# HGRN2 in a decoder trunk: stacked exponents, cross scores in place of a state, weights rounded on GpSimd, and a new order of calls

## What is computed

```python
q, fz, i, g = jnp.split(x @ w_in, 4, axis=-1)
q = silu(q); f = lower_bound + (1 - lower_bound) * sigmoid(fz)
log_f = jnp.log(f); k = 1 - f
# in each of 8 heads of width 128, b = cumsum(log_f) over tokens:
#   out[t] = sum over s <= t of (sum_k q[t,k] k[s,k] exp(b[t,k] - b[s,k])) v[s]
o = rms_norm(o, g_norm) * silu(g)
return o @ w_o
```

## Time and profile before

| | |
|---|---|
| median of 3 runs | 995.34 us (995.27 to 995.46) |
| the profiled execution's own time | 994.82 us |
| its span, first to last instruction | 993.3 us |
| PE busy | 982.4 us, 99% of the span |
| DVE, ACT, POOL busy | 711.2, 501.1, 38.4 us |
| phase C, roughly | 645 to 798 us of the span |
| TensorE clock granted | 0.999 of full speed |

### The profile page before, as it was taken

One profiled execution on the slowest core, in us unless ns is written; L12 is line 12 of the kernel. 1 busy time (PEld: TensorE's weight loads), 2 busy tenths in 40 slices (PEclk: granted clock), 3 DMA queues, 4 the chain that ended last, 5 costly groups with the idle time before them and its releaser, 6 DMA issues.

```text
span 993.3 us, 13958 instructions
## 1 busy us (share of the span) xinstructions
PE 982.4 (99%) x5116; PEld 829.9 (84%) x5116; DVE 711.2 (72%) x960; ACT 501.1 (50%) x571; POOL 38.4 (4%) x63
## 2 busy tenths in 40 slices
PE   9999999999999999999999999999999999999996
PEld 7888888888888888888888888888888888888885
DVE  5686667785879666668786666788877877565665
ACT  6663544346547544532444343358978535444430
POOL 0100000000210000000000000000001100000000
PEclk9999999999999999999999999999999999999999
DMA  8687655552756656563666464734233657656521
GB/s 296 221 285 243 210 168 193 170 194 103 251 202 235 220 175 205 172 233 122 215 214 210 164 211 168 236 111 145 85 128 125 215 174 239 214 167 210 165 101 42
DMA packets 129255, 184.72 MB, mean 186 GB/s; under 512 B 5952, under 2 KB 104784, under 8 KB 129088
## 3 DMA queue, kind: packets, MB, share of 16 engines
q1 hardware_dynamic: 126032, 173.56, 52.2%
q0 software_dynamic: 2624, 10.11, 2.9%
q10 hardware_dynamic: 560, 0.52, 0.2%
HBM read 183.13 MB, written 1.05 MB: 185 GB/s over the span
## 4 chain that ended last, share of the span: by engine, by line
PE 93%; DVE 2%; ACT 2%; DMA 1%; issue 0%; POOL 0%; DVEq 0%; SPq 0%; ACTq 0%
PE psum L1527 24%; PE psum L1501 17%; PE psum L1503 17%; PE psum L1502 17%; PE psum L1531 12%; PE psum L1975 1%; DMA raw<-in_ffn_w_in 1%; ACT w_hi L429 1%; PE psum L1496 1%; PE psum L1960 1%; PE psum L1644 1%; DVE w_lo L853 0%; PE psum L1940 0%; PE psum L1711 0%; DVE stats L893 0%
## 5 line engine op out<-in xcount | busy, mean ns | idle before, releaser
L853 DVE TENSOR_TENSOR w_lo<-raw,w_hi 128x2048 fp32r<-128x2048 f32 x161 | 367.4, 2287 | 40.7 <-ACT w_hi L429 40.1
L1527 PE MATMUL psum<-xT,w_hi 128*128 128x512 f32 x1024 | 358.5, 396 | 0.0
L429 ACT CAST w_hi<-raw 128x2048 fp32r<-128x2048 f32 x161 | 303.9, 1909 | 26.7 <-DMA raw<-in_ffn_w_in 15.6
L1531 PE MATMUL psum<-xT,w_lo 128*128 128x256 f32 x1024 | 275.7, 280 | 0.0
L1527 PEld LDWEIGHTS psum<-xT,w_hi 128*128 128x128 f32 x1024 | 190.4, 188 | 41.3
L1531 PEld LDWEIGHTS psum<-xT,w_lo 128*128 128x128 f32 x1024 | 192.9, 188 | 5.4
L944 DVE TENSOR_REDUCE ffn_tok<-psum 128x256 f32<-128x512 f32 x128 | 82.4, 686 | 152.3 <-PE psum L1527 152.3
L1501 PE MATMUL psum<-w_hi,xT 128*128 128x512 f32 x447 | 178.8, 400 | 0.8 <-DVE xT L874 0.7
L1503 PE MATMUL psum<-w_hi,xT 128*128 128x512 f32 x447 | 174.7, 391 | 0.0
L1502 PE MATMUL psum<-w_lo,xT 128*128 128x512 f32 x447 | 174.4, 390 | 0.0
L463 ACT ACTIVATE ffn_tok<-ffn_tok 128x256 f32<-128x256 f32 x64 | 26.8, 418 | 233.6 <-DVE ffn_tok L944 233.6
(11 more groups left out here) (197 smaller groups left out, 692.5 us busy)
## 6 DMA issues: line engine op xcount, KB each, us to landing
raw<-in_ffn_w_in SPq DMA_DIRECT2D x170, 512.0 KB, 4.7
raw<-in_ffn_w_out SPq DMA_DIRECT2D x88, 512.0 KB, 3.9
raw<-in_c_w_in SPq DMA_DIRECT2D x32, 512.0 KB, 4.5
raw<-in_ab_w_in SPq DMA_DIRECT2D x16, 512.0 KB, 4.8
raw<-in_ab_w_o SPq DMA_DIRECT2D x8, 512.0 KB, 3.8
raw<-in_c_w_o SPq DMA_DIRECT2D x8, 512.0 KB, 3.9
ln_gb<-in_ln_gain POOLq DMA_DIRECT2D x6, 512.0 KB, 6.5
ln_gb<-in_ln_bias POOLq DMA_DIRECT2D x6, 512.0 KB, 7.3
```

The source lines that it names most:

```text
L429: nc.scalar.copy(w_hi[:, n % RING], raw[:, slot]).then_inc(hi_ready, 1)
L853: nc.vector.tensor_tensor(w_lo[:, n % RING], raw[:, n % RAW], w_hi[:, n % RING].bitcast(F32), ALU.subtract).then_inc(lo_ready, 1)
L1527: return nc.tensor.matmul(dst, w_hi[:, slot, cs], xT_both[:, kk].rearrange("p a f -> p (a f)"), start=kk == 0, stop=kk == KB - 1)
L1531: return nc.tensor.matmul(dst[:, 0:SEQ], w_lo[:, slot, cs], xT_hi[:, kk], start=False, stop=False)
```

## The change

Five parts, all in phase C.

1. Stacked exponents. The high part of log f for tokens 0 to 63 of a tile and the low part of the same tokens are put on partitions 0 to 63 and 64 to 127 of one tensor, those of tokens 64 to 127 in the other. The tables in `decay` are repeated on both halves, and one matmul with 128 rows and 256 columns gives the sum that took two before. The whole-tile sums are now formed from one half-tile table and a multiplication by the total of the other half, on DVE.
2. Cross scores. In place of the transpose, its copy, the state and its copy, one matmul (L2034 in the new kernel) gives the scores between the first tile's keys and the second tile's queries; ACT copies it to `cross`, and `head_outputs` multiplies it with the first tile's values.
3. The rounding of log f is two ACT instructions and the subtraction two DVE instructions, each on half the partitions.
4. The splits 2 to 16 of phase C (15 units) are rounded by POOL in place of ACT. DVE still subtracts.
5. A new order of the calls on PE, ACT and DVE, and an order on POOL with the rms norms between its splits. `gam` is copied to `ln_gb` ahead of the first `queries`; POOL no longer waits for the norm ahead of phase C to end.

```diff
@@ build @@
+        KQT_AFTER_KQT = (1, 3)
+        CROSS_BEFORE_KQT = (0, 0, 2, 0, 3, 4, 6, 7)
+        KQT_BEFORE_CROSS = (2, 2, 4, 5, 6, 6, 7, 8)
@@ scalar: log_decay, head_exp, head_cross @@
-                nc.scalar.copy(hT_hi[:, par].rearrange("p (t f) -> p t f", t=TT), logf).then_inc(S["logf_hi"], 1)
+                for b in range(2):
+                    rs = slice(64 * b, 64 * b + 64)
+                    ins = nc.scalar.copy(decay_sums[b][rs, par].rearrange("p (t f) -> p t f", t=TT), logf[rs])
+                ins.then_inc(S["logf_hi"], 1)
...
-                if b == 0:
-                    nc.scalar.activation(EXP_FULL, EXP_FULL, ACT.Exp)
-                group = EXP[b].rearrange("p b l t f -> p b (l t f)")
-                ins = nc.scalar.activation(group, group, ACT.Exp)
+                nc.scalar.activation(EXP_USED[b], EXP_USED[b], ACT.Exp).then_inc(S["decays_ready"], 1)
-            def head_klT(hd):
-                act.wait_ge(S["klT_done"], hd + 1)
-                nc.scalar.copy(klT, bank[0][:, 0:P]).then_inc(S["klT_ready"], 1)
-            def head_state(hd):
-                act.wait_ge(S["state_done"], hd + 1)
-                nc.scalar.copy(state, bank[0][:, 0:P]).then_inc(S["state_ready"], 1)
+            def head_cross(hd):
+                act.wait_ge(S["cross_done"], hd + 1)
+                if hd:
+                    act.wait_ge(S["head_done"], hd)
+                nc.scalar.copy(cross, bank[0][:, 0:P]).then_inc(S["cross_ready"], 1)
@@ vector: upper_factors (new; the rest of head_factors is lower_factors) @@
+                nc.vector.tensor_tensor(fac[:, 0, :, P // 2:], EXP_ENDS,
+                                        bass.AP(a.tensor, a.offset + P // 2, [a.ap[0], (3 * P, 2), (1, P // 2)]),
+                                        ALU.mult)
+                for t in range(TT):
+                    nc.vector.scalar_tensor_tensor(out=fac[:, 0, t, 0:P // 2], in0=exponent(1, t)[:, 0],
+                                                   scalar=EXP_TOTALS[t], in1=a[:, 3 * t, 0:P // 2],
+                                                   op0=ALU.mult, op1=ALU.mult)
@@ gpsimd (new) @@
+            def split_hi(n):
+                pool.wait_ge(raw_landed[n % RAW], 32 * (n // RAW))
+                used, value, _ = used_by[n - RING]
+                pool.wait_ge(used, value)
+                pool.wait_ge(hi_ready, n)
+                nc.gpsimd.tensor_copy(w_hi[:, n % RING], raw[:, n % RAW]).then_inc(hi_ready, 1)
@@ tensor: head_exponents, head_levels, head_outputs @@
-                for t in range(TT):
-                    full = decay[:, t, 0]
-                    nc.tensor.matmul(EXP_FULL[:, t], hi[:, t, hs], full, start=True, stop=False)
-                    nc.tensor.matmul(EXP_FULL[:, t], lo[:, t, hs], full, start=False, stop=True)
-                for b, (l0, l1) in enumerate(FACTORS):
+                for group, (l0, l1) in enumerate(FACTORS):
                     for t in range(TT):
-                        for a in (hi, lo):
-                            for half in range(2):
-                                rs = slice(64 * half, 64 * half + 64)
-                                ins = nc.tensor.matmul(EXP[b][:, half, :, t], a[rs, t, hs], decay[rs, t, l0:l1, rs],
-                                                       start=a is hi, stop=a is lo)
+                        for b in range(2):
+                            both = decay_sums[b][:, g % 2].rearrange("p (t f) -> p t f", t=TT)
+                            ins = nc.tensor.matmul(EXP[group][:, b, :, t], both[:, t, hs], decay[:, t, b, l0:l1],
+                                                   start=True, stop=True)
...
-                        nc.tensor.transpose(bank[0][:, 0:P], fac[:, 0, 0], ident[:]).then_inc(S["klT_done"], 1)
-                pe.wait_ge(S["klT_ready"], hd + 1)
-                pe.wait_ge(S["val_ready"], 2 * (hd // 4) + 1)
-                nc.tensor.matmul(bank[0][:, 0:P], klT, val[hd // 4][:, 0, hs], start=True, stop=True
-                                 ).then_inc(S["state_done"], 1)
+                        nc.tensor.matmul(bank[0][:, 0:P], fac[:, 0, 0], fac[:, 0, 1], start=True, stop=True
+                                         ).then_inc(S["cross_done"], 1)
...
-                nc.tensor.matmul(bank[1][:, P:2 * P], fac[:, 0, 1], state, start=False, stop=True
+                nc.tensor.matmul(bank[1][:, P:2 * P], cross, v[:, 0, hs], start=False, stop=True
```

More of the change, by code:

```diff
@@ L281, in build @@
         scT = region(6656, TT, P)
-        state = region(6912, P)
+        cross = region(6912, P)
         kq_tmp = region(8192, 2, P)
-        klT = region(7040, P)
         level_mask = region(8448, NL * P // 4).bitcast(U8).rearrange("p (n f) -> p n f", n=NL)
@@ L1238, in mix_c @@
                 decays(2, 1)
-                head_factors(3)
-                own = head_own(3)
+                upper_factors(3)
+                scores = head_own(3)
+                lower_factors(3)
+                split(7)
+                scores = upper_scores(3, scores)
+                logf_split(2)
+                lower_scores(3, scores)
                 split(8)
-                head_scores(3, own)
-                logf_split(2)
-                own = head_own(4)
                 split(9)
-                head_factors(4)
+                upper_factors(4)
@@ L1256, in mix_c @@
+                scores = head_own(5)
+                lower_factors(5)
                 logf_split(3)
+                scores = upper_scores(5, scores)
+                lower_scores(5, scores)
                 split(11)
[L1258 to L1259 removed]
                 split(12)
[L1261 removed]
+                upper_factors(6)
+                lower_factors(6)
+                scores = head_own(6)
+                scores = upper_scores(6, scores)
@@ new lines, in logf_split, with level_factors @@
+                ins.then_inc(S["logf_lo"], 1)
+            def level_factors(hd, l):
+                a, half = kqT[:, hd % 2], LEVELS[l]
+                for t in range(TT):
+                    if half < P // 2:
+                        ins = nc.vector.tensor_tensor(
+                            blocks(fac[:, 1 + l], t * half, P, half),
+                            exponent(1 + l, t).rearrange("p b (s j) -> p s b j", s=2),
+                            blocks(a, t * (P + half), 2 * P + (-half if t else half), half), ALU.mult)
+                        continue
+                    for b in range(2):
+                        queries = b != t
+                        ins = nc.vector.tensor_tensor(
+                            fac[:, 1 + l, int(queries), t * half:(t + 1) * half], exponent(1 + l, t)[:, b],
+                            a[:, 2 * queries + t, b * half:(b + 1) * half], ALU.mult)
+                return ins
@@ L2050, in shape_constants @@
     mask += [below, below[::-1, ::-1]]
-    decay = []
-    for t, sums in enumerate(([keys_to_end] + levels, [a[::-1, ::-1] for a in [queries_from_start] + levels])):
-        for half, a in zip((None,) + LEVELS + (None, None), sums):
-            if half is None or half == P // 2:
-                decay.append(a)
-                continue
-            b, kind, j = np.arange(P) // 64, np.arange(P) // 32 % 2, np.arange(P) % 32
-            at = b * 64 + j // half * 2 * half + (kind ^ t) * half + j % half
-            decay.append(a[:, at])
-    for i, a in enumerate(decay + mask):
-        c[:, C_DECAY + i * P:C_DECAY + (i + 1) * P] = a
+    decay = np.zeros((P, TT, 2, N_DECAY, 64), np.float32)
+    for t in range(TT):
+        for n, (half, a) in enumerate(zip((None,) + LEVELS + (None, None), [ends] + levels)):
+            if n == 0 and t == 1:
+                a = (p >= f) & (f >= P // 2)
+            elif t == 1:
+                a = a[::-1, ::-1]
+            at = np.arange(P)
+            if half is not None and half < P // 2:
+                b, kind, j = at // 64, at // 32 % 2, at % 32
+                at = b * 64 + j // half * 2 * half + (kind ^ t) * half + j % half
+            for b in range(2):
+                rs = slice(64 * b, 64 * b + 64)
+                decay[:, t, b, n] = np.tile(a[rs][:, at[rs]], (2, 1))
+    c[:, C_DECAY:C_MASK] = decay.reshape(P, -1)
+    for i, a in enumerate(mask):
+        c[:, C_MASK + i * P:C_MASK + (i + 1) * P] = a
     return c
```

339 lines of the change are left out of this document (173 added, 166 removed).

## The result

The changed kernel takes 1003.06 us (1001.31 to 1003.37, 4 runs), the kernel before 995.35 (995.27 to 995.46, 4 runs): ratio 1.0074, interval 1.0062 to 1.0087. It is 7.7 us slower. The forecast was 991.2, its range ended at 1001. The profiled execution took 1003.37 us, its span is 1001.8.

The account below looks back on a forecast made before the run. PE was taken as the bound, with DVE's 16.9 us of idle time in the heads second. 994.82 less 7.5 saved on PE plus 3.4 of waits gave 990.7 profiled, 991.2 as a median, range 986.5 to 1001.

Parts of the forecast that it names:

- 5.8 + 0.9 us: PE's work over eight heads: stacked exponents save 5.8 us, cross scores in place of transpose and state 0.9.
- the 0.8: PE at head 7: two waits on ACT's copies go, saving 0.8 us, bounds 0.3 to 0.8.
- ACT's 26.8 us: Heads' stretch: ACT loses 13 roundings and 8 copies, 26.8 of 85.8 us, making exponentials and copies earlier.
- rival C: Nothing to tell from before, 993.3 to 997.3 us: holds of 1.16 to 1.56 each or a tight head's chain; chance 0.13.
- it costs nothing unless a rounding holds DVE, which is one more 1 us: Ahead of the heads' stretch: a 2.29 us split fills DVE's 2.32 us idle time; a hold would add 1 us.
- h = 0.95 us: Heads' stretch: each POOL rounding holds DVE for half of 1.9 us, ten times, 9.5 us in all.
- 3.4: Heads' stretch: PE waits 3.4 us, as DVE needs 96.9 us where PE offers 93.5.
- 10 h - 6.1: Heads' stretch: PE's waits in us for ten roundings that each hold DVE for h.
- D: Heads' stretch: DVE held for the whole of ten 1.9 us roundings, PE waits 12.9, median 1000.7 us; chance 0.20.
- A: Heads' stretch: DVE hardly held, PE keeps its 7.5 us, median 987.8, range 986.5 to 989.4; chance 0.30.

Follow-up runs that it names:

- the one that only writes: The changed kernel with POOL's 15 roundings replaced by writes of a constant to the same 128 x 2048 words, reading nothing: 990.07 us.
- the held-back kernel: The changed kernel with roundings 2 to 4 on ACT, first values copied earlier, POOL's other twelve each waiting for DVE's factors or score copies: 990.03 us.
- without the waits: The changed kernel with roundings 2 to 4 on ACT, first values copied earlier, POOL's other twelve not made to wait for DVE: 994.61 us.
- last experiment: The kernel before, its order kept, with stacked exponents, cross scores, roundings 2 to 4 on ACT, 5 to 16 on POOL waiting for DVE's factors or copies: 994.24 us.
- first experiment: The changed kernel with splits 2 to 16 rounded by ACT again instead of POOL: 999.44 us.
- the kernel with values first: The changed kernel with roundings 2 to 16 on ACT and the first values copied ahead of the second tile's sigmoids: 996.44 us.

## Why the prediction was wrong

1. **PE's own work: right.** Forecast 5.8 + 0.9 us; by the balance 6.4 in the changed kernel, 6.9 in the one that only writes, 5.8 with the exponents alone. The two waits at head 7 are gone too, as the 0.8 had it (1.35 with restarts).

2. **ACT's 26.8 us cost nothing, and POOL's rounding takes 1.9 us: right** (1.90 undisturbed, 2.11 in the mean).

3. **The new order costs nothing: wrong, 3.6 us.** I took ACT's copies to be earlier everywhere and gave the order no price but a share in rival C. The first copy of values stands behind sigmoids that wait for PE (1.4 us), and two waits for DVE in the heads (0.50 at 713.53, 1.11 at 772.32, 2.1 with restarts) stand in the kernel that only writes too.

4. **"it costs nothing unless a rounding holds DVE, which is one more 1 us": the step that failed most.** I counted ten roundings in the heads' stretch and put those ahead of it at nothing, 1 us at most, since DVE had idled there. Four ran there. The new list had filled DVE's idle time with a split, and the layer norm ahead of the phase, which I had not looked at, is held as well. The holds there made 4.0 us of waits (1.1, 1.0, 1.8), 4.8 with the restarts, and 1.7 us at the lower clock: 6.5 us.

5. **What a rounding costs DVE, h = 0.95 us: too small, and the smaller part of the miss.** I took it halfway between nothing and all, because no row showed DVE as the loser. It is 1.26 us, 18.9 for fifteen. The halfway value was argued from the share of DVE's time that is exposed, a third for splits. But an instruction of 0.28 us that met a rounding at 665.54 took 1.98, 1.70 more, and ended 0.14 us behind it. So the hold goes by what is left of POOL's instruction, not by the share of time. In the heads eight waits are 6.2 us, 8.3 with restarts, where I had 3.4. Two of them, 2.1, are the order's (3). The six that are left, 6.2, fit my own formula, 10 h - 6.1, which gives 6.5 for the measured h; that is 2.8 more than the forecast.

6. **The rivals.** D named the mechanism and its sign, and had 0.20. Its price of 1.9 us a rounding was too high, and its place, the heads' stretch, misses the larger part. That its 1000.7 is near the 1003.06 is in part luck: the price too high made up for the place left out. A's world, in which DVE is hardly held, is real when POOL doesn't read, or reads beside PSUM instructions: 990.07 and 990.03 us, 0.7 and 0.6 above A's range.

So the forecast for the profiled execution, 990.7, missed 1003.4 by 12.7 us: 6.5 are the holds ahead of the heads with the lower clock behind them, 3.6 the new order, 2.8 the size of h in the heads. The rest, -0.2, is PE's own work and the waits at head 7. One of the four runs took 1001.31 at a mean clock of 0.999 where the others have 0.996, so the 1.7 us of the clock may not be in every run; even that run lies above the range.

The Trainium skill (SBUF — State Buffer, "Who interferes with whom") says that the exclusion goes both ways, for a whole instruction, and that a GpSimd instruction which only writes doesn't contend with a DVE instruction with two SBUF inputs. Both are borne out here: a decay instruction went from 0.42 to 1.79 us at 670.31, and beside the writes the weight splits are at 2285 ns and the decay instructions at 418. The prediction gave it half weight for want of a row.

What stays open: how the 13.0 us divide between holds of the decay instructions and of the weight splits; which call of the new order makes the two waits for DVE in the heads (they were not moved by themselves); and what of the gain of the held-back kernel over the changed one (13.0 us) is due to moving three roundings back to ACT; without the waits these three and the values' copy together gave 8.4.

## What to carry to other kernels

When work moves to GpSimd, list the DVE instructions with two SBUF operands that can be under way beside it, and price each meeting at the rest of the GpSimd instruction, not at a share of time; then look first at the place with the least slack, here the start of the phase, and at what runs ahead of it. If the work must go there, put it beside DVE work that reads PSUM, with a wait close ahead of it and nothing slow between that wait and it, or cut it in pieces (6.6 us here). And a shorter instruction sequence in front of the bound engine (the stacked exponents) is worth only what its operands' makers can keep up with: 5.8 us saved, 0.8 seen.

## What was not expected of the hardware

- POOL's write of 128 x 2048 without a read leaves DVE's instructions with two SBUF inputs alone, but holds L1361, which reads one SBUF tensor (`ident`) and a column of `kq_own` and writes SBUF: 532 ns in the mean where it was 283, its longest 1.86 us. PE did not wait for it.
- After an idle stretch of PE of 1.84 us (changed kernel), 1.83 (last experiment) and 2.96 (first experiment) the granted clock stood at 0.57 to 0.59 for about 4 us. After 1.92 and 2.22 us, at 760.86 and 764.65 of the kernel with values first, and 1.70 in the one with only POOL's roundings, it did not fall. In the last experiment five runs took 992.6 to 993.2 us at a mean clock of 0.998 to 0.999, and six 994.2 to 994.6 at 0.996 to 0.997; the profiled run, which had the fall, is one of the six. So one fall is worth some 1.4 us there, an estimate.
- A restart of PE after a wait costs 0.27 us beyond the idle time that the profile names (669.11 of the changed kernel).
